# Down tiles of 256 inner rows by 1024 outputs in an expert stage, run as a loop of two turns

## What is computed

```python
def moe_swiglu(h, w_router, w_gate, w_up, w_down):
    logits = (h @ w_router).astype(jnp.float32)
    top_val, top_idx = lax.top_k(logits, TOP_K)
    top_w = jax.nn.softmax(top_val, axis=-1)
    gates = jnp.sum(jax.nn.one_hot(top_idx, N_EXPERTS, dtype=jnp.float32) * top_w[..., None], axis=-2)
    out = jnp.zeros_like(h)
    for e in range(N_EXPERTS):
        y = swiglu(h, w_gate[e], w_up[e], w_down[e])     # (silu(h @ w_gate) * (h @ w_up)) @ w_down
        out = out + gates[..., e:e + 1].astype(h.dtype) * y
    return out
```

## Time and profile before

| | us |
|---|---|
| median of the runs shown | 3089.13 |
| these runs | 3087.59, 3099.47, 3089.13 |
| the profiled execution | 3093.76 |
| its span | 3091.6 |
| start of the first gather to the last spread | 662 to 1606 |

### The profile page before, as it was taken

The page is one execution under the profiler, slowest core; times in us unless marked ns, Lnnn a source line. Parts: engine busy times, 40 slices in busy tenths (PEclk is TensorE's granted clock), DMA queues, the critical chain, the costliest instruction groups (busy, mean ns, idle before and its releaser), DMA issues. The chain is left out here.

```text
span 3091.6 us, 70624 instructions
## 1 busy us (share of the span) xinstructions
PE 2844.8 (92%) x31472; PEld 2104.7 (68%) x31472; DVE 621.8 (20%) x1701; ACT 395.5 (13%) x1066; POOL 32.7 (1%) x46
## 2 busy tenths in 40 slices
PE   5889999989999999999988987888999999888999
PEld 2577866669989999999975546774544444445883
DVE  0121001121001001001011136662222211223331
ACT  0111001011000000000001213331111100122110
POOL 0000000000000000000000000000000000000000
PEclk9899999999999999999999887888999999989999
DMA  8783443349999999999971110000222212311442
GB/s 343 308 345 123 153 159 136 109 181 341 379 369 386 390 377 388 385 374 389 390 287 68 55 41 2 2 2 27 82 82 70 80 50 74 128 48 55 150 150 82
DMA packets 80421, 584.39 MB, mean 189 GB/s; under 512 B 8912, under 2 KB 8912, under 8 KB 10064
## 3 DMA queue, kind: packets, MB, share of 16 engines
q1 hardware_dynamic: 79920, 580.15, 48.7%
q10 hardware_dynamic: 288, 1.05, 0.1%
HBM read 580.11 MB, written 1.05 MB: 188 GB/s over the span
## 5 line engine op out<-in xcount | busy, mean ns | idle before, releaser
L1412 PE MATMUL ps<-arena,ring 128*64 128x88 f32 x14336 | 553.8, 239 | 25.9 <-issue 22.3
L1412 PEld LDWEIGHTS ps<-arena,ring 128*64 128x64 f32 x14336 | 547.6, 137 | 31.2 <-issue 29.2
L2524 PE MATMUL ps<-hT,ring 128*128 128x256 f32 (+2 forms) x1472 | 456.8, 473 | 5.6 <-ACT hT L464 3.4
L2524 PEld LDWEIGHTS ps<-hT,ring 128*128 128x128 f32 x1472 | 276.0, 192 | 185.2 <-issue 166.3
L352 PE MATMUL ps<-ring,arena 128*128 128x512 f32 x896 | 388.4, 594 | 4.4 <-DVE small L996 4.4
L352 PEld LDWEIGHTS ps<-ring,arena 128*128 128x128 f32 x896 | 170.4, 191 | 216.5 <-issue 214.9
L1504 PE MATMUL ps<-arena,ring 128*64 128x88 f32 x7168 | 280.1, 239 | 20.1 <-issue 19.9
L1504 PEld LDWEIGHTS ps<-arena,ring 128*64 128x64 f32 x7168 | 274.0, 137 | 30.2 <-issue 30.2
L198 PE MATMUL ps<-hT,ring 128*128 128x256 f32 (+1 forms) x608 | 191.3, 475 | 8.2 <-ACT arena L749 4.0
L198 PEld LDWEIGHTS ps<-hT,ring 128*128 128x128 f32 x608 | 116.5, 193 | 80.9 <-issue 71.4
L1521 ACT ACTIVATE arena<-ps 128x88 f32<-128x88 f32 x224 | 54.8, 245 | 828.0 <-PE ps L1412 828.0
(11 more groups left out here) (508 smaller groups left out, 2264.8 us busy)
## 6 DMA issues: line engine op xcount, KB each, us to landing
ring<-in_stream SPq DMA_DIRECT2D x547, 1024.0 KB, 7.0
par<-in_params SPq DMA_DIRECT2D x1, 3397.0 KB, 28.9
h<-in_x ACTq DMA_DIRECT2D x2, 512.0 KB, 8.3
cx<-in_ctx SPq DMA_DIRECT2D x2, 512.0 KB, 29.5
out<-h SPq DMA_DIRECT2D x4, 256.0 KB, 2.0
par<-in_params SPq DMA_DIRECT2D x1, 941.0 KB, 6.5
```

The source lines that it names most:

```text
L1412: last = nc.tensor.matmul(ps[m:m + 64, up_bank[j], half * P:half * P + CAP], w[:, k, half * P + m:half * P + m + 64], hTe[:, k, :], start= ...
L2524: last = nc.tensor.matmul(ps[:, 2 * BANKS_CONV[f % RING] + half, tok], w[:, k, half * P:half * P + P], hT[:, k, tok], start=(k == 0), stop ...
```

## The change

The same 14 MB of down weights of an expert are cut otherwise: 14 tiles of 256 inner rows by all 1024 outputs. A tile has 2 row groups by 8 groups of outputs by 2 halves, again 32 matmuls with the same weight block, and writes banks 6 and 7 in turn. `start=True` is gone from them; two matmuls of one column each (identity by a column of the identity, into column 127 of banks 6 and 7, which nobody reads) begin the sums. For experts 1 to 7 the 14 tiles are a loop of two turns over 7 tiles. Since the instructions of both turns must read the same place in `hid`, GpSimd copies row groups 14 to 27 onto groups 0 to 13, two groups after each tile of the first turn, and counts in `moe_moved[d]`, for which PE waits ahead of tile `d`. DVE's two copies to `yT` both wait for the last tile. Expert 0 stays written out. The host packs the tiles to match; the overflow path is adapted and stays skipped.

```diff
+        moe_moved = [sem(f"moe_moved{d}") for d in range(F_MOE // 4)]
...
+        def down_products(w, d):
+            for j in range(2):
+                for q in range(KT):
+                    for m in (0, 64):
+                        last = nc.tensor.matmul(ps[m:m + 64, 6 + q // 4, (q % 4) * P:(q % 4) * P + CAP],
+                                                w[:, j, q * P + m:q * P + m + 64], hid[:, 2 * d + j, :],
+                                                start=False, stop=(d == kd - 1 and j == 1), skip_group_check=True)
+            last.then_inc(tile_used.sem, 1)
...
                 for half in range(2):
-                    for d in range(kd):
-                        k0 = at + nf + half * kd + d
-                        pe.wait_ge(landed[slot(k0)], wait_of(k0))
-                        w = ring[:, slot(k0), :].rearrange("p (k n) -> p k n", k=4)
-                        for j in range(4):
-                            for q in range(4):
-                                for m in (0, 64):
-                                    last = nc.tensor.matmul(ps[m:m + 64, 6 + half, q * P:q * P + CAP],
-                                                            w[:, j, q * P + m:q * P + m + 64],
-                                                            hid[:, 4 * d + j, :], start=(d == j == q == 0),
-                                                            stop=(d == kd - 1 and j == 3), skip_group_check=True)
-                        last.then_inc(tile_used.sem, 1)
+                    nc.tensor.matmul(ps[:, 6 + half, P - 1:P], ident, ident[:, 0:1], start=True, stop=False,
+                                     skip_group_check=True)
+                for d in range(2 * kd if e == 0 else 0):
+                    pe.wait_ge(landed[slot(nf + d)], wait_of(nf + d))
+                    down_products(ring[:, slot(nf + d), :].rearrange("p (k n) -> p k n", k=2), d)
+                if e:
+                    with pe.Fori(0, 2) as part:
+                        for d in range(kd):
+
+                            pe.wait_ge(landed[slot(nf + d)], part * 16 + (16 * (per // RING) * e + wait_of(nf + d)))
+                            pe.wait_ge(moe_moved[d], part + e)
+                            down_products(ring[:, slot(nf + d), :].rearrange("p (k n) -> p k n", k=2), d)
...
+        @block.gpsimd
+        def _(pool):
+            for d in range(kd):
+                pool.sem_inc(moe_moved[d], 1)
+            for e in range(1, EXPERTS):
+                hid_made(pool, e * nf + nf - 1)
+                for d in range(kd):
+                    pool.wait_ge(tile_used.sem, moe_t0 + e * per + nf + d + 1)
+                    nc.gpsimd.tensor_copy(hid[:, 2 * d:2 * d + 2, :], hid[:, 2 * (kd + d):2 * (kd + d) + 2, :])\
+                        .then_inc(moe_moved[d], 1)
...
-                    dve.wait_ge(tile_used.sem, moe_t0 + e * per + nf + (half + 1) * kd)
+                    dve.wait_ge(tile_used.sem, moe_t0 + e * per + per)
...
-        both_halves(i["moe_w_down"][0, e])
+        rows(i["moe_w_down"][0, e], 0, D, 2)
```

More of the change, by code:

```diff
@@ L1635, in _ @@
                     pe.wait_ge(over_out, e * 4 + 4)
[L1636 to L1640, removed]
+                    for d in range(2 * kd):
+                        k0 = nf + d
+                        pe.wait_ge(over_landed[k0 % 2], e * (8 * per) + 16 * (k0 // 2 + 1))
+                        w = oring[:, k0 % 2, :].rearrange("p (k n) -> p k n", k=2)
+                        for half in range(2):
                             for t in range(TT):
-                                for j in range(4):
+                                for j in range(2):
                                     last = nc.tensor.matmul(ps[:, 2 * half + t, :],
-                                                            ohid[:, 4 * d + j, t * P:t * P + P], w[:, j, :],
-                                                            start=(d == j == 0), stop=(d == kd - 1 and j == 3))
-                            last.then_inc(over_used, 1)
+                                                            ohid[:, 2 * d + j, t * P:t * P + P],
+                                                            w[:, j, half * 512:half * 512 + 512],
+                                                            start=(d == j == 0), stop=(d == 2 * kd - 1 and j == 1))
+                        last.then_inc(over_used, 1)
                 pe.wait_ge(over_out, EXPERTS * 4 + 4)
@@ L1686, in _ @@
                     for half in range(2):
-                        dve.wait_ge(over_used, e * per + (2 + nf + (half + 1) * kd))
+                        dve.wait_ge(over_used, e * per + (2 + per))
                         for t in range(TT):
```

## The result

The changed kernel takes 3067.3 us (median of 5 runs, 3060.83 to 3071.59), before 3089.13 us. The ratio is 0.9923, with a 95% interval of 0.9899 to 0.9947. The profiled execution took 3067.69 us, 26.1 us less than that of before.

A forecast was written before the change was run, and what follows sets the result against it. The prediction took PE to be the bound, its idle time being late fetches of its own instruction blocks. Terms of -19.8, -6.2, +3.5 and +0.7 gave -21.8 us, taken from the median 3089.13: 3067.3 us, range 3058 to 3086.

The follow-up runs named there:

- e7: The changed kernel with its up loop as 2 turns over 14 tiles instead of 4 turns over 7; 3167.24 us.
- e6: The kernel before with the up loop of experts 1 to 7 written out, 28 tiles each; 3175.2 us.
- e10: The changed kernel with every weight tile loaded by two transfers of half the columns, waits counting to 32 instead of 16; 3096.98 us.
- e5: The kernel before with only the first half of each weight tile's columns loaded in the expert stage, save the last tiles; 3035.06 us.
- e11: The changed kernel with each of GpSimd's copies made 16 times, one after the other, before it counts; 3164.41 us.

## What to carry to other kernels

Where PE works off small matmuls at full pitch while the DMA engines are full, the length of the written-out program has a price: look for idle times by "issue" every 256 instructions and at the same time for packets on PE's instruction queue, and turn written-out repetitions into loops short enough to be kept. A loop too long to be kept may be worse than none: e7 took 3167 us, and the changed kernel with its up loop written out would take 3151 by an estimate from e6 (3067 + 84). What remains of the lateness follows how full the weight stream is just there, so work without loads should stand ahead of new code; moving 1.7 us of it was worth more here (8.8 us) than looping expert 0.

## What was unexpected of the hardware

- A loop of 3.5 blocks of 256 instructions was replayed without a single packet. One of 7.1 blocks was fetched anew in its second turn in six of seven cases, with a stop of up to 7.83 us at the branch back, and in the seventh replayed without a packet (e7).
- Weight loads in pieces of 4 KB per partition instead of 8 KB made more instruction blocks late: 38.7 us in 39 gaps instead of 20.7 in 22, 3096.98 us (e10).
- Half the bytes in the weight stream made 42 of 44 gaps or more vanish with the same code (e5).
- The same program's gaps in one stretch of the stage came to 4.1 us in one execution and 7.3 us in another.
- After PE had stood for 7.83 us the granted clock was 0.76 over the next 9 us (e7); between waits of 2 to 4 us it fell to 0.50 (e11).
